# Latent attention scores from rounded values and rests: three single passes in place of one full-precision product, in a two-block transformer kernel

## The chip, the cores and the metric

The kernel runs on one core of a Trainium2 chip. Five engines work side by side: TensorE (matrix products and transposes, results into PSUM), ScalarE (one function or copy over a tile), VectorE (elementwise work and reductions), GpSimd and SyncE, which here starts the transfers of weights from memory. Each engine runs its own queue in order and waits on semaphores. The metric is the device time in microseconds of one execution.

## What is computed

Two transformer blocks of two layers each over 256 tokens of width 1024. The change touches only one part of the first block, latent attention with 8 heads whose queries and keys have 96 features (64 from a projection, 32 rotated):

```python
def latent_attention(c_q, c_kv, k_rope, w_qb, w_kvb, q_norm_g, kv_norm_g):
    q = jnp.einsum('bsr,re->bse', rms_norm(c_q, q_norm_g), w_qb).reshape(b, s, MLA_HEADS, MLA_NOPE_DIM + MLA_ROPE_DIM)
    ...
    k = jnp.concatenate([k_nope, jnp.broadcast_to(k_r, (b, s, MLA_HEADS, MLA_ROPE_DIM))], -1)
    o = blocked_attention(q, k, v, (MLA_NOPE_DIM + MLA_ROPE_DIM) ** -0.5)

def blocked_attention(q, k, v, scale):
    ...
        sc = jnp.einsum('bqhd,bkhd->bhqk', qi, k, preferred_element_type=jnp.float32) * scale
        p = jax.nn.softmax(sc, axis=-1).astype(v.dtype)
        return jnp.einsum('bhqk,bkhd->bqhd', p, v)
```

Everything is float32.

## The kernel before

Weights stream through three slots of 2048 columns. ScalarE writes each piece's rounded value (`whi`, type float32r) and VectorE the rest (`wlo` = piece minus `whi`); there are four slots of each. A weight product is then three single passes: rounded by rounded, rounded by rest, rest by rounded. ScalarE's `split_to` (L1184) waits for the transfer and for a free slot (`w_used`, given by TensorE when it has read a piece to the end); VectorE's `split_to` (L1708) waits for ScalarE.

The order on each engine is written out by hand. In the stage of the latent heads (points "ml") TensorE mixes attention with weight products. `filler` (L559) hands out a share of such products at each call of `fill`, and `mark` notes which weight products have ended there. ScalarE and VectorE call `catch` at the same points; it evicts what has ended and parts the next pieces of weights.

The heads go in groups g = 0 to 3 of two, heads 2g and 2g+1, and a fifth round finishes the last pair. Each round of TensorE is: the scores of the two heads (L835), the turn of head 2g+2 (`turn_latent`, L800: four full-precision transposes at L804, queries and keys, into 96 partitions of PSUM bank 6), products, the transposes of the probabilities of the group before (`turn_probs`, L630, at L638), products, the turn of head 2g+3, the second transposes of probabilities, products, and `mix_pair` (L641, at L648: probabilities by values). Heads 0 and 1 are turned ahead of the rounds. In the second layer the same happens again.

There is only one bank for a turned head. So `turn_latent` of a head waits for `qk_out` of the head before it, with which VectorE says that it has copied bank 6 to `qk` (L1919, buffer 0 for even heads, 1 for odd ones). The scores of a head wait for its own `qk_out` and for the exponentials that last used their bank.

VectorE in a round: `normalise_pair` of the group before (L1943), `maxima` of both heads (L1926, at L1929 and L1930), `qk_out` of head 2g+2, `catch`, `catch`, `qk_out` of head 2g+3, `catch`, and the rest of the mixed pair. ScalarE in a round: the exponentials of both heads (`exp_pair`, L1315, at L1324), `catch`, `probs_out` (L1328, at L1332: the turned probabilities out of PSUM), `catch`, `probs_out`, `catch`, `pair_hi`.

Of the kernel before, what the change touches and what calls it, by code (L numbers as in the profile page):

```python
# [11 lines left out]
ALU = mybir.AluOpType  # L12
# [50 lines left out]
    "first_sum", "windows_in", "rotated", "subln", "lam", "lam_exp",  # L63
    "qk_turned", "qk_out", "scored", "negm", "exped", "heads_out",
    "probs_in", "probs_turned", "probs_out", "heads_mixed", "pairs_mixed", "pair_hi", "pair_out",
# [4 lines left out]
Sems = namedtuple("Sems", SEMS)  # L70
Tensors = namedtuple("Tensors", [n for n, _, _ in SBUF] + ["ps", "down", "cw", "sgw", "brow", "xTh", "xTl"])
Kernel = namedtuple("Kernel", "nc t out m s raws leads free size first after call bank halves seen")
# [51 lines left out]


def by_columns(ap):

    return ap.rearrange("p (r w c) -> p w r c", r=4, w=4)
# [11 lines left out]
def build(nc, t, out):  # L140
    first, after, call, size = {}, {}, {}, []
    for name, pieces in gemm_names():
        first[name], after[name], call[name] = len(size), len(size) + len(pieces), len(call) + 1
        size += pieces
    with ExitStack() as ctx:
        sb = [ctx.enter_context(nc.sbuf_tensor(name, shape, dt)) for name, shape, dt in SBUF]
        ps = ctx.enter_context(nc.psum_tensor("ps", [P, 8, 512], F32))
        named = dict(zip([n for n, _, _ in SBUF], sb))
        flat = named["rpb"][:].rearrange("p a b c -> p (a b c)")
        m = Tensors(*sb, ps, ps[:, 4:8, :].rearrange("p (t n) w -> p t (n w)", t=2),  # L150
                    flat[:, 0:NSTEP * 16].rearrange("p (c f k) -> p c f k", c=NSTEP, f=4),
                    flat[:, D:2 * D].rearrange("p (h q) -> p h q", h=8), flat[:, 2 * D:2 * D + 640], named["xT"][:, :, 0, :], named["xT"][:, :, 1, :])
        s = Sems(*[ctx.enter_context(nc.semaphore(name)) for name in SEMS])
        k = Kernel(nc, t, out, m, s, (s.raw0, s.raw1, s.raw2), (s.lead0, s.lead1, s.lead2), (s.free0, s.free1, s.free2), size, first, after, call,
                   {}, [], {})
        tensor_program(k)
        sync_program(k)
        pool_program(k)
        scalar_program(k)
        vector_program(k)  # L160
# [240 lines left out]
def tensor_program(k):  # L401
# [282 lines left out]
    for L in range(DEPTH):  # L684
# [144 lines left out]
        for g in range(5):  # L829
            if g < 4:  # L830
                for h in (2 * g, 2 * g + 1):
                    PE.wait_ge(s.qk_out, g0 + h + 1)
                    PE.wait_ge(s.exped, h0 + 2 * g)
                    for th in range(2):
                        mm = PE.matmul(ps[:, 3 + h % 2, th * S:(th + 1) * S], m.qk[0:96, h % 2, th * P:(th + 1) * P],  # L835
                                       m.qk[0:96, h % 2, S:2 * S], start=True, stop=True)
                    mm.then_inc(s.scored, 1)
# [341 lines left out]
def scalar_program(k):  # L1179
# [135 lines left out]
    def exp_pair(h0, p_free, g, scale, biased=False, heads=(0, 1)):  # L1315

        for h in [2 * g + j for j in heads]:
# [8 lines left out]
            e.then_inc(s.exped, 1)  # L1326

    def probs_out(p0, i, m_free, width=2 * S):  # L1328
        AC.wait_ge(s.probs_turned, p0 + i + 1)
        if m_free > 0:  # L1330
            AC.wait_ge(s.pairs_mixed, m_free)
        AC.activation(m.probT[:, i % 2, 0:width], ps[:, 5, 0:width], ACT.Copy).then_inc(s.probs_out, 1)  # L1332
# [41 lines left out]
    for L in range(DEPTH):  # L1374
# [65 lines left out]

        for i in (6, 9):
            catch(1, L, "ml", "pre", i)
        blocks_hi(m.bTh, 4, 3, gain=lambda kt: m.pcol[:, 6:7])
# [3 lines left out]
        for g in range(5):  # L1447
            if g < 3:
                exp_pair(h0, p0 + 2 * g - 2, g, 96 ** -0.5)
            if g == 3:  # L1450
                exp_pair(h0, p0 + 2 * g - 2, g, 96 ** -0.5, heads=(0,))
            catch(1, L, "ml", g, 1, ahead=0 if g else SPLIT)
            if g:
                probs_out(p0, 2 * g - 2, m0 + g - 1)
            if g == 3:
                exp_pair(h0, p0 + 2 * g - 2, g, 96 ** -0.5, heads=(1,))
            catch(1, L, "ml", g, 2)
            if g:
                probs_out(p0, 2 * g - 1, m0 + g - 1)
# [238 lines left out]
def vector_program(k):  # L1698
# [217 lines left out]

    def qk_out(rows, buf):
        DV.wait_ge(s.qk_turned, n.up("groups"))
        DV.tensor_copy(m.qk[0:rows, buf, :], ps[0:rows, 6, :]).then_inc(s.qk_out, 1)  # L1919

# [89 lines left out]
    for L in range(DEPTH):  # L2010
# [65 lines left out]
        n.up("probs", 4)  # L2076
        qk_out(P, 0)
        catch(1, L, "df", "pre", 4)
# [5 lines left out]
        for g in range(5):  # L2084
# [4 lines left out]
            if g < 3:  # L2089
                qk_out(P, (g + 1) % 2)  # L2090
            if g == 4:
# [9 lines left out]
        n.up("probs", 8)  # L2101
        qk_out(96, 0)
        catch(1, L, "ml", "pre", 6)
        qk_out(96, 1)
        catch(1, L, "ml", "pre", 9)
# [9 lines left out]
        for g in range(5):  # L2115
            if g:
                normalise_pair(h0, g - 1)
            if g < 4:
                maxima(h0, g, 96 ** -0.5)
            if g < 3:  # L2120
                qk_out(96, 0)
            catch(1, L, "ml", g, 1, ahead=0 if g else SPLIT)
            catch(1, L, "ml", g, 2)
            if g < 3:
                qk_out(96, 1)
            catch(1, L, "ml", g, 3, ahead=SPLIT - 1)
            if g:
                pair_lo(g - 1)
# [380 lines left out]
```

## Time and profile before

| | before |
|---|---|
| median of 3 runs | 1452.88 us (1452.18 to 2392.74) |
| the profiled execution | 1452.48 us, span 1451.2 us |
| TensorE busy (products) | 1436.1 us, 99% |
| VectorE busy | 1040.1 us, 72% |
| ScalarE busy | 813.7 us, 56% |
| share of the transfer engines | 53.8% for the weights' queue |

A page of the profile tells how long each engine was busy in the span. Matmuls are pipelined: a row's duration runs from its start to an end that is modelled, and neighbours overlap, so what a pass takes of TensorE is read from the distance of two starts. A full-precision product appears as two records. In the time lines below times count from the start of the span.

### The profile page before, as it was taken

What the parts mean: (1) busy time and instruction counts of PE and PEld (TensorE: products, weight loads), DVE (VectorE), ACT (ScalarE), POOL (GpSimd) and SP (SyncE); (2) the same over time, 40 slices, a digit from 0 to 9 for tenths busy, and PEclk for the clock granted to TensorE, in tenths of its full rate; (3) what the DMA queues carried; (4) which work ended last, traced back from release to release, by engine and by line L of the source; (5) the groups of instructions that cost most, each with busy time, mean ns of one, the idle gap of its engine ahead of it and who ended that gap; (6) DMA issues with size and microseconds to landing.
All of it is one profiled execution on the core that took longest, in us unless ns stands there. A gap on an engine that the chain in (4) does not pass through costs nothing.

```text
span 1451.2 us, 19722 instructions
## 1 busy us (share of the span) xinstructions
PE 1436.1 (99%) x7721; PEld 1208.5 (83%) x7721; DVE 1040.1 (72%) x1423; ACT 813.7 (56%) x1177; POOL 62.2 (4%) x100
## 2 busy tenths in 40 slices
PE   8999999999999999999999999999999999999999
PEld 6788878888887888887888888788888888888888
DVE  5766876855557556875865556877988868788886
ACT  5565554354443565754454444676655657775563
POOL 1010000000001000000100000210000012000000
PEclk9999999999999999999999999999999999999999
DMA  8754635565665464642756565436556644456651
GB/s 271 250 191 147 217 131 170 171 210 183 200 212 187 156 204 133 217 147 92 254 183 219 184 198 174 147 109 209 174 189 198 217 134 160 139 177 202 197 186 58
DMA packets 172684, 261.09 MB, mean 180 GB/s; under 512 B 9520, under 2 KB 111568, under 8 KB 172336
## 3 DMA queue, kind: packets, MB, share of 16 engines
q1 hardware_dynamic: 171296, 255.18, 53.8%
q0 software_dynamic: 1152, 4.65, 0.9%
q8 instruction: 61, 1.00, 0.3%
q14 instruction: 31, 0.25, 0.1%
q10 hardware_dynamic: 144, 0.01, 0.0%
HBM read 256.66 MB, written 1.05 MB: 178 GB/s over the span
## 4 chain that ended last, share of the span: by engine, by line
PE 92%; DVE 5%; ACT 1%; POOL 1%; issue 1%; DMA 0%; DVEq 0%; ACTq 0%
PE ps L458 16%; PE ps L534 12%; PE ps L536 11%; PE ps L535 11%; PE ps L459 9%; PE ps L428 7%; PE ps L432 6%; PE ps L430 6%; PE ps L461 2%; DVE wlo L1714 1%; PE ps L835 1%; PE ps L486 1%; PE ps L638 1%; DVE bn L1721 1%; PE ps L1076 1%; DVE x L1773 1%
## 5 line engine op out<-in xcount | busy, mean ns | idle before, releaser
L1714 DVE TENSOR_TENSOR wlo<-raw,whi 128x2048 fp32r<-128x2048 f32 (+1 forms) x234 | 519.6, 2229 | 224.2 <-ACT whi L1192 224.2
L1192 ACT ACTIVATE whi<-raw 128x2048 fp32r<-128x2048 f32 (+1 forms) x234 | 434.4, 1865 | 139.9 <-PE ps L536 52.2
L458 PE MATMUL ps<-xT,whi 128*128 128x512 f32 x1008 | 356.4, 395 | 0.0
L459 PE MATMUL ps<-xT,wlo 128*128 128x256 f32 x1152 | 311.2, 280 | 0.0
L534 PE MATMUL ps<-whi,xT 128*128 128x512 f32 (+3 forms) x640 | 250.4, 391 | 2.2 <-DVE xT L1792 1.2
L536 PE MATMUL ps<-whi,xT 128*128 128x512 f32 (+3 forms) x640 | 242.0, 378 | 0.0
L535 PE MATMUL ps<-wlo,xT 128*128 128x512 f32 (+3 forms) x640 | 241.4, 377 | 0.0
L458 PEld LDWEIGHTS ps<-xT,whi 128*128 128x128 f32 x1008 | 189.0, 188 | 42.1
L459 PEld LDWEIGHTS ps<-xT,wlo 128*128 128x128 f32 x1152 | 217.4, 189 | 6.1
L534 PEld LDWEIGHTS ps<-whi,xT 128*128 128x128 f32 x640 | 120.3, 188 | 25.1 <-issue 5.2
L536 PEld LDWEIGHTS ps<-whi,xT 128*128 128x128 f32 x640 | 120.2, 188 | 22.6
L535 PEld LDWEIGHTS ps<-wlo,xT 128*128 128x128 f32 x640 | 120.6, 188 | 19.0
L428 PE MATMUL ps<-whi,aTh 128*128 128x512 f32 x300 | 93.0, 391 | 0.0
L430 PE MATMUL ps<-wlo,aTh 128*128 128x512 f32 x300 | 92.7, 390 | 0.0
L432 PE MATMUL ps<-whi,aTl 128*128 128x512 f32 x300 | 92.6, 390 | 0.0
L2370 DVE SCALAR_TENSOR_TENSOR proj<-proj,rpb 128x255 f32<-128x255 f32 x160 | 70.2, 480 | 2.2 <-ACT proj L1636 0.7
L432 PEld LDWEIGHTS ps<-whi,aTl 128*128 128x128 f32 x300 | 56.3, 188 | 12.0
L430 PEld LDWEIGHTS ps<-wlo,aTh 128*128 128x128 f32 x300 | 56.3, 188 | 11.8
L428 PEld LDWEIGHTS ps<-whi,aTh 128*128 128x128 f32 x300 | 55.7, 188 | 10.4
L1513 ACT ACTIVATE prob<-ps 128x512 f32<-128x512 f32 x36 | 21.6, 599 | 73.2 <-PE ps L461 73.2
L461 PE MATMUL ps<-xT,whi 128*128 128x512 f32 x144 | 53.8, 396 | 0.0
L1636 ACT ACTIVATE proj<-proj,rpb 128x256 f32<-128x256 f32 x80 | 43.5, 591 | 13.7 <-DVE proj L2386 11.5
(244 smaller groups left out, 1962.5 us busy)
## 6 DMA issues: line engine op xcount, KB each, us to landing
raw<-in_w_in SPq DMA_DIRECT2D x120, 512.0 KB, 4.8
raw<-in_w_ffn_in SPq DMA_DIRECT2D x88, 512.0 KB, 4.9
raw<-in_w_up SPq DMA_DIRECT2D x88, 512.0 KB, 4.8
raw<-in_w_ffn_out SPq DMA_DIRECT2D x44, 512.0 KB, 4.4
raw<-in_w_down SPq DMA_DIRECT2D x44, 512.0 KB, 4.5
raw<-in_w_branch SPq DMA_DIRECT2D x24, 512.0 KB, 4.8
raw<-in_w_out SPq DMA_DIRECT2D x16, 512.0 KB, 4.2
raw<-in_w_o SPq DMA_DIRECT2D x16, 512.0 KB, 4.6
```

The lines of the kernel that those rows point to most:

```text
L428: PE.matmul(o, ah, hi[:, j, b], start=first and kt == 0, stop=False)
L430: PE.matmul(o, ah, lo[:, j, b], start=False, stop=False)
L432: mm = PE.matmul(o, al, hi[:, j, b], start=False, stop=last and j == c - 1 and i == len(kts) - 1)
L458: PE.matmul(ps[:, b, :], hi, m.xT[:, kt], start=kt == 0, stop=False)
L459: mm = PE.matmul(ps[:, b, 0:S], lo, m.xTh[:, kt], start=False, stop=False)
L461: mm = PE.matmul(ps[:, b, :], hi, m.xT[:, kt], start=False, stop=True)
L534: PE.matmul(o, ah, hi[:, j, :], start=kt == 0, stop=False)
L535: PE.matmul(o, ah, lo[:, j, :], start=False, stop=False)
L536: mm = PE.matmul(o, al, hi[:, j, :], start=False, stop=end)
L1192: AC.activation(m.whi[:, i % SPLIT, 0:w], m.raw[:, slot, 0:w], ACT.Copy).then_inc(s.w_hi, 1)
L1714: DV.tensor_tensor(m.wlo[:, i % SPLIT, 0:w], m.raw[:, slot, 0:w], m.whi[:, i % SPLIT, 0:w].bitcast(F32), ALU.subtract).then_inc(s.w_lo, 1)
L2370: a = DV.scalar_tensor_tensor(out=conv[:, f, to], in0=src[:, f, of], scalar=m.cw[:, c, f, tap:tap + 1], in1=conv[:, f, to], op0=ALU.mult, ...
```

## The change

The copy of a turned head by VectorE is replaced by two steps. ScalarE copies bank 6 as float32r, which rounds it, into `lath` (`latent_hi`), and gives the new semaphore `qk_hi`. VectorE waits for that and writes the bank minus the rounded value into `latl` (`latent_lo`), then gives `qk_out`, as its copy did. `lath` lies where `qk` lay, `latl` in the half of `rpb` that held the values of the neighbourhood heads. Each product of the scores (128 queries by 256 keys, in full precision) becomes three single passes: rounded queries by rounded keys, rest of queries by rounded keys, rounded queries by rest of keys. The product of the two rests is left out, as in the weight products.

```diff
@@ tensor_program, latent heads
                 for h in (2 * g, 2 * g + 1):
                     PE.wait_ge(s.qk_out, g0 + h + 1)
                     PE.wait_ge(s.exped, h0 + 2 * g)
+                    hi, lo = latent_parts(m, h % 2)
                     for th in range(2):
-                        mm = PE.matmul(ps[:, 3 + h % 2, th * S:(th + 1) * S], m.qk[0:96, h % 2, th * P:(th + 1) * P],
-                                       m.qk[0:96, h % 2, S:2 * S], start=True, stop=True)
+                        o, qh = ps[:, 3 + h % 2, th * S:(th + 1) * S], hi[:, th * P:(th + 1) * P]
+                        PE.matmul(o, qh, hi[:, S:2 * S], start=True, stop=False)
+                        PE.matmul(o, lo[:, 0, th, :], hi[:, S:2 * S], start=False, stop=False)
+                        mm = PE.matmul(o.rearrange("p (t s) -> p t s", t=2), qh, lo[:, 1], start=False, stop=True)
                     mm.then_inc(s.scored, 1)
@@ scalar_program
+    def latent_hi(buf):
+
+        h = n.up("latent")
+        AC.wait_ge(s.qk_turned, h + 8 * ((h + 7) // 8))
+        AC.activation(latent_parts(m, buf)[0], ps[0:96, 6, :], ACT.Copy).then_inc(s.qk_hi, 1)
+
@@ scalar_program, latent heads
-        for i in (6, 9):
-            catch(1, L, "ml", "pre", i)
+        latent_hi(0)
+        catch(1, L, "ml", "pre", 6)
+        latent_hi(1)
+        catch(1, L, "ml", "pre", 9)
...
             if g == 3:
                 exp_pair(h0, p0 + 2 * g - 2, g, 96 ** -0.5, heads=(0,))
+            if g < 3:
+                latent_hi(0)
             catch(1, L, "ml", g, 1, ahead=0 if g else SPLIT)
...
             catch(1, L, "ml", g, 2)
+            if g < 3:
+                latent_hi(1)
             if g:
                 probs_out(p0, 2 * g - 1, m0 + g - 1)
@@ vector_program
+    def latent_lo(buf):
+
+        n.up("groups")
+        hi, lo = latent_parts(m, buf)
+        DV.wait_ge(s.qk_hi, n.up("qk_hi"))
+        DV.tensor_tensor(lo, ps[0:96, 6, :].rearrange("p (a t s) -> p a t s", a=2, t=2),
+                         hi.bitcast(F32).rearrange("p (a t s) -> p a t s", a=2, t=2), ALU.subtract).then_inc(s.qk_out, 1)
@@ vector_program, latent heads: the four calls
-                qk_out(96, 0)
+                latent_lo(0)
```

On ScalarE the new copy stands behind the four exponentials of a group. This is the first group of the first layer before, from the exponentials (`prob<-ps,negm`) over the gate (`gate<-gate`) and a piece of weights (`whi<-raw`) to the exponentials of the next group:

```order
L1324 ACTIVATE prob,rs<-ps,negm 128x256 [waits probs_turned,negm]
L1324 ACTIVATE prob,rs<-ps,negm 128x256
L1324 ACTIVATE prob,rs<-ps,negm 128x256 [waits probs_turned,negm]
L1324 ACTIVATE prob,rs<-ps,negm 128x256
L1291 ACTIVATE gate<-gate 128x512 [waits free2]
L1192 ACTIVATE whi<-raw 128x2048 [waits w_used,raw2]
```

The same place in the changed kernel:

```order
L1337 ACTIVATE prob,rs<-ps,negm 128x256 [waits probs_turned,negm]
L1337 ACTIVATE prob,rs<-ps,negm 128x256
L1337 ACTIVATE prob,rs<-ps,negm 128x256 [waits probs_turned,negm]
L1337 ACTIVATE prob,rs<-ps,negm 128x256
L1345 ACTIVATE lath<-ps 96x512 [waits qk_turned]
L1304 ACTIVATE gate<-gate 128x512 [waits free2]
L1345 ACTIVATE lath<-ps 96x512 [waits qk_turned]
L1205 ACTIVATE whi<-raw 128x2048 [waits w_used,raw2]
```

The copy of head 2 has come in between the exponentials and the gate, that of head 3 between the gate and the weights. In group 2 of the changed kernel the copy stands ahead of the probabilities' copy (`probT<-ps`) and of the weights:

```order
L1337 ACTIVATE prob,rs<-ps,negm 128x256 [waits probs_turned,negm]
L1337 ACTIVATE prob,rs<-ps,negm 128x256
L1345 ACTIVATE lath<-ps 96x512 [waits qk_turned]
L1351 ACTIVATE probT<-ps 128x512 [waits pairs_mixed,probs_turned]
L1205 ACTIVATE whi<-raw 128x2048 [waits w_used,raw1]
L1345 ACTIVATE lath<-ps 96x512 [waits qk_turned]
L1351 ACTIVATE probT<-ps 128x512 [waits pairs_mixed,probs_turned]
```

On VectorE nothing moves; the copy of bank 6 becomes a subtraction in the same place. In group 0 of the first layer it stood between the maxima and the gate's addition, before:

```order
L1929 TENSOR_REDUCE negm<-ps 128x2 [waits scored]
L1930 TENSOR_SCALAR negm<-negm 128x2 [waits dve_step]
L1919 COPY qk<-ps 96x512 [waits qk_turned]
L1849 TENSOR_TENSOR gate<-ps,vec 128x512 [waits th0_sum,gate_b]
L1919 COPY qk<-ps 96x512 [waits qk_turned]
```

and now:

```order
L1962 TENSOR_REDUCE negm<-ps 128x2 [waits scored]
L1963 TENSOR_SCALAR negm<-negm 128x2 [waits dve_step]
L1951 TENSOR_TENSOR latl<-ps,lath 96x4x128 [waits qk_hi]
L1874 TENSOR_TENSOR gate<-ps,vec 128x512 [waits th0_sum,gate_b]
L1951 TENSOR_TENSOR latl<-ps,lath 96x4x128 [waits qk_hi]
```

What it waits for is now ScalarE (`qk_hi`) and no longer TensorE (`qk_turned`).

## Rows read from the trace of the kernel before

**Rows 1.** The page's busy times: engine, us, share of the span, instructions.
```profile
PE 1436.1 (99%) x7721; PEld 1208.5 (83%) x7721; DVE 1040.1 (72%) x1423; ACT 813.7 (56%) x1177; POOL 62.2 (4%) x100
```

**Rows 2.** The chain that ended last, share of the span by engine.
```profile
PE 92%; DVE 5%; ACT 1%; POOL 1%; issue 1%; DMA 0%; DVEq 0%; ACTq 0%
```

**Rows 3.** TensorE's waits for weight rests: us in total, times, longest.
```profile
PE ps L534 <- DVE wlo L1714: 0.4, 1, 0.4
```

**Rows 4.** Window, length, busy us of PE, PEld, DVE, ACT, POOL; clock, transfers.
```profile
177.00:217.00 40.00, 40.00 (x208) 32.05 (x208) 31.74 (x55) 20.90 (x48) 0.00 (x0) 1.00 0.40 132
```

**Rows 5.** TensorE's time line (start, us, line, out<-in, xcount), head 3, group 1.
```profile
183.52 0.60 PE L804 MATMUL ps<-ident,proj 128*96 128x128 f32 x4
...
186.02 1.89 PE L835 MATMUL ps<-qk 96*128 96x256 f32 x8
187.75 0.60 PE L804 MATMUL ps<-ident,proj 128*96 128x128 f32 x4
```

**Rows 6.** Time line, single passes of 256 columns in the second block.
```profile
1150.54 0.28 PE L453 MATMUL ps<-xT,whi 128*128 128x256 f32 x1
1150.55 0.19 PEld L454 LDWEIGHTS ps<-xT,wlo 128*128 128x128 f32 x1
1150.66 0.28 PE L454 MATMUL ps<-xT,wlo 128*128 128x256 f32 x1
...
1150.78 0.28 PE L455 MATMUL ps<-xT,whi 128*128 128x256 f32 x1
```

**Rows 7.** Time line of VectorE and ScalarE, end of group 0's exponentials.
```profile
182.04 0.68 DVE L1919 COPY qk<-ps 96x512 f32<-96x512 f32 x1
...
183.09 0.21 ACT L1324 ACTIVATION_READ_ACCUMULATOR prob<-ps,negm 128x1 f32 x1
183.10 0.69 DVE L1849 TENSOR_TENSOR gate<-ps,vec 128x512 f32<-128x512 f32 x1 [0.38 <-PE ps L536]
...
183.83 0.63 ACT L1291 ACTIVATE gate<-gate 128x512 f32<-128x512 f32 x1 [0.52 <-DVE gate L1849]
```

**Rows 8.** Time line, a transpose that waited for VectorE.
```profile
150.50 0.88 DVE L1960 SCALAR_TENSOR_TENSOR prob<-prob,ri 128x256 f32<-128x256 f32 x2
...
151.44 0.66 PE L638 MATMUL ps<-ident,prob 128*128 128x128 f32 x4
```

**Rows 9.** Time lines of the three engines, group 2 and scores of group 3.
```profile
202.85 0.21 ACT L1324 ACTIVATION_READ_ACCUMULATOR prob<-ps,negm 128x1 f32 x1
202.94 0.61 ACT L1332 ACTIVATE probT<-ps 128x512 f32<-128x512 f32 x1
...
203.70 0.60 PE L804 MATMUL ps<-ident,proj 128*96 128x128 f32 x4
...
205.38 2.29 DVE L1714 TENSOR_TENSOR wlo<-raw,whi 128x2048 fp32r<-128x2048 f32 x1 [1.59 <-ACT whi L1192]
...
207.75 1.99 PE L835 MATMUL ps<-qk 96*128 96x256 f32 x8
...
210.96 0.39 PE L534 MATMUL ps<-whi,xT 128*128 128x512 f32 x1
211.19 0.39 PE L535 MATMUL ps<-wlo,xT 128*128 128x512 f32 x1
```

**Rows 10.** Time lines of the three engines, group 1 and scores of group 2.
```profile
189.80 0.21 ACT L1324 ACTIVATION_READ_ACCUMULATOR prob<-ps,negm 128x1 f32 x1
...
192.79 0.60 PE L804 MATMUL ps<-ident,proj 128*96 128x128 f32 x4
...
196.69 0.68 DVE L1919 COPY qk<-ps 96x512 f32<-96x512 f32 x1
196.84 1.99 PE L835 MATMUL ps<-qk 96*128 96x256 f32 x8
```

**Rows 11.** Second layer, the two rows that answer to group 2 above.
```profile
649.92 0.61 ACT L1332 ACTIVATE probT<-ps 128x512 f32<-128x512 f32 x1
...
650.67 0.60 PE L804 MATMUL ps<-ident,proj 128*96 128x128 f32 x4
```

## Prediction: where TensorE gains, and where it waits for the copy

> **What bounds the kernel now.** I read the page's busy times first: TensorE is busy 1436.1 us, 99% of the span [rows 1]. The chain that ended last is 92% TensorE [rows 2]. So the time is the sum of what TensorE runs, plus the moments in which it stands still: work taken from TensorE shortens the run, work added to another engine costs nothing until TensorE waits for it. Next I read the waits of TensorE: the largest one for weight rests is 0.4 us, once [rows 3]. Last I read the time of the latent heads: from 177 to 217 us TensorE is busy 40.00 of 40.00 us, VectorE 31.74, ScalarE 20.90, at a granted clock of 1.00, the upper level of 2.4 GHz [rows 4]. TensorE can't be filled further here, VectorE has little room, ScalarE has room on average. What matters is when ScalarE is free, since a new step on it now stands between a transpose and the scores.
>
> **Scores: less TensorE work.** There are 4 groups of two heads in each of 2 layers, 8 groups. A group's four full-precision products are eight records, and from the first of them (186.02) to the transposes behind them (187.75) it takes 1.73 us [rows 5]. After the change a group is 2 heads x 2 halves x 3 = 12 single passes of 128x256 with a weight load each. The same kind of run stands in the second block: passes at 1150.54, 1150.66 and 1150.78, so 0.12 us each [rows 6]. 12 x 0.12 = 1.44, a gain of 0.29 us a group, 2.3 us in all. The floor of a pass is half of a record of the present scores, since two passes lie in each record of 1.73/8 = 0.216 us: 0.108, which would gain 0.43 a group, 3.5 in all. I take 0.12, because the loads lie beside it there as they will here. A pass of single precision behind full-precision work starts no later than a full-precision one does, so I book nothing for the switch (at most 0.1 a group, 0.8 in all).
>
> **One rule that speaks against it.** The rows show a load beginning at 1150.55, 0.01 us after the product ahead of it began, and lasting 0.19, while products go on every 0.12 [rows 6]: loads lie beside products. The Trainium skill, in "TensorE: Matmul & The Clock Gate", section "The mechanism", says that a weight load overlaps running matmuls only where the row groups differ, which they don't here. Twelve loads in place of eight would then be a loss. The trace does not agree, so the sum goes by 0.12.
>
> **Parting: what is added.** VectorE copied a 96x512 bank in 0.68 us [rows 7]. Now it subtracts, reading the bank and the rounded value; the row nearest to that is the 128x512 addition out of PSUM, 0.69 [rows 7]. Its work doesn't change, by these two (bounds 0.6 and 0.9: a third more for writing in pieces of 128 columns, which no row shows). ScalarE gets 16 copies of 96x512 from PSUM. The copy of 128x512 out of PSUM takes 0.61 [rows 9]; I take 0.60, bounds 0.5 and 0.8 (the same spread). As work this is hidden (ScalarE 20.90 of 40). As a step in a chain it isn't: the bank is read by ScalarE first, VectorE waits for that, and TensorE may not turn the next head until the rest is written.
>
> **Where the copy comes too late: group 0.** ScalarE executes in order, and the copy of head 2g+2 is queued behind the four exponentials of group g. In group 0 TensorE turned head 3 at 183.52 [rows 5]; VectorE had copied head 2 at 182.04 to 182.72 [rows 7], so nobody waited. Now: the last read of the exponentials starts at 183.09 [rows 7], and the next ScalarE instruction follows 0.09 behind such a read (202.85 to 202.94 [rows 9]), so at 183.18. The exponentials don't move, since VectorE's maxima ahead of them stand behind weight rests. The copy ends at 183.78, the rest goes from 183.81 to 184.50, and TensorE starts 0.06 behind the end of what it waits for (VectorE ends 150.50 + 0.88, TensorE starts 151.44 [rows 8]): 184.56. It would have been ready at 183.52 - 0.29 = 183.23. **Stall 1.33 us**, and TensorE is now 1.04 later than before.
>
> Is anything behind that late too? On VectorE the gate addition of 183.10 comes at 184.42, ScalarE's gate of 183.83 at 185.15 [rows 7], and the copy of head 3 behind it ends at 186.26, its rest at 186.98. Scores of group 1 are due at 186.02 + 1.04 = 187.06: just covered, by 0.02. In group 1, where TensorE is 1.04 late up to the scores and 0.75 behind them, the exponentials end at about 191.0 (189.80 + 0.21 [rows 10], plus 1.04), the rest of head 4 at 192.3, and TensorE turns head 5 at 192.79 + 0.75 = 193.54 [rows 10]. Covered by 1.2 us. The rest of head 5 stands behind two weight rests, as its copy did (196.69 [rows 10]), and moves with TensorE by 0.75: it ends at 198.12. The scores of group 2, 196.84 before [rows 10], start at 197.59 with head 4 and want head 5 at 197.59 + 0.72 = 198.31. Covered by 0.13.
>
> **Group 2.** TensorE is 1.04 - 0.29 - 0.29 = 0.46 later than before and turns head 7 at 203.70 + 0.46 = 204.16 [rows 9]. VectorE has been running without a pause and carries its 0.75 of delay, so the exponentials' last read starts at 202.85 + 0.75 = 203.60 [rows 9]; the copy runs 203.69 to 204.29, the rest to 205.00, TensorE starts at 205.05. **Stall 0.89 us.** Behind it ScalarE has the probabilities' copy (202.94 before, now 204.2) and then the weights' rounded piece, so the weight rest of 205.38 comes 1.24 later [rows 9]. Who waits for that piece? It is the first of the second gate half; TensorE opens the half ahead of it at 210.96 and spends 48 passes of 0.23 us on it (210.96 to 211.19), so it is wanted from 222 on, and there are some 13 us. The rest of head 7 comes right behind that weight rest (205.38 + 1.24 + 2.2 = 208.8) and ends at 209.5, and its scores are due at 207.75 + 1.35 + 0.72 = 209.8 [rows 9]. Covered. Group 3 parts no heads and gives 0.29 back. After the latent heads VectorE and ScalarE have pauses in which they catch up, but TensorE has none, and what it lost stays lost.
>
> **Sum.** A layer: -4 x 0.29 + 1.33 + 0.89 = +1.06 us. The second layer runs the same order at the same distances: TensorE's turn of head 7 at 650.67 and ScalarE's copy at 649.92 [rows 11] stand 446.97 and 446.98 behind those of rows 9. So twice: **+2.1 us** (gain 2.3, stalls 4.4). The profiled execution took 1452.48 us, 1.3 more than its span; the median of the runs is 1452.88. 1452.88 + 2.1 = 1455.0.
>
> **Rivals.**
> 1. *The copy is in time, the gain stays.* That wants ScalarE's copy and VectorE's rest to be done 1.3 us sooner in group 0. Against it: the exponentials start only at VectorE's negated maxima, which don't move, and the queue is fixed. For it: only that TensorE's waits are read from ends that are modelled. Time: 1452.9 - 2.3 = 1450.6, with the floor of 0.108 a pass 1449.4. This is the case of a gain.
> 2. *More stalls than two.* Covers of 0.02 (scores of group 1) and 0.13 (head 5's scores) are thin. If the copy takes 0.8 and the rest 0.9, each of the two stalls grows by 0.4 and the scores of group 1 wait 0.4: 1.2 a layer more, 1457.4. With the other cover gone as well (0.3) and 0.1 at each switch of precision it is 1459 to 1460.
> 3. *Loads don't lie beside these passes* (the slow side beyond 2%). A pass would take 0.19 + 0.12 = 0.31, a group 3.7 us in place of 1.73, 8 x 2.0 = 16 us more, 1469 without stalls and about 1473 with them. From 0.48 us a pass on (1.73 + 4 us a group) it would be slower by over 2%. Against it stand rows 6. The rule of the Trainium skill named above would put the run on this side; by the same page's figures (sections "LDWEIGHTS (loading the stationary operand)" and "Back-to-back issue gap": 107 ns for 128 columns of weights, 109 ns for 256 columns of product) a group would be estimated at 12 x 0.216 = 2.6 us.
> 4. *Nothing can be told*: gain and stalls cancel, 1452.9.
>
> **How the numbers follow.** Forecast with two stalls a layer (1453.5 to 1457) 0.60; rival 2 0.17; rival 1 0.14; rival 4 0.06; rival 3 0.03. The range of 1451.0 to 1459.5 leaves out most of rival 1, rival 3 and the end of rival 2. 2% is 29 us, about what a measurement of this kernel can tell from no change: all cases but the far end of rival 3 lie within it. Faster by over 2% 0.005, within 0.985, slower 0.01.
>
> **What the changed profile would show.** The twelve passes of a group over 1.44 us, 0.12 apart. TensorE's weight load of the turns of heads 3 and 7 idle before it for 1.3 and 0.9 us, released by VectorE's subtraction, in both layers, and no such wait at heads 1, 2, 4, 5, 6. ScalarE's copy at about 0.60, the subtraction at about 0.69, and VectorE waiting for ScalarE some 1 to 2 us ahead of the subtractions of heads 2, 4 and 6. I would be wrong if the turn of head 3 had no wait (then the time is near 1452 or under), if waits stood ahead of the scores themselves, or if passes stood 0.2 apart.

## The result, and the profile after

The changed kernel takes 1455.21 us (median of 15 runs, 1454.72 to 1456.57), the kernel before 1452.31 (median of 15). The ratio is 1.0021, 95% interval 1.0014 to 1.0028: 2 to 4 us more, 3.0 as the ratio has it. One run of the kernel before took 2392.74 us, far outside the rest, and is left out of the ratio; why it did is not known. The profiled execution took 1455.96 us with a span of 1454.6.

The page's busy times after (engine, us, share of the span, instructions), and the chain that ended last:

```profile
PE 1435.4 (99%) x7753; PEld 1209.6 (83%) x7753; DVE 1040.3 (72%) x1423; ACT 820.9 (56%) x1193; POOL 62.2 (4%) x100
PE 88%; DVE 7%; ACT 2%; issue 1%; DMA 1%; POOL 1%; SPq 0%; DVEq 0%; ACTq 0%
```

TensorE has 32 products more (8 groups x 12 passes in place of 8 records) and is busy 0.7 us less than in [rows 1]. That 0.7 is not the gain of the passes: rows that end in a wait run on into it by their modelled ends, so each of the two stages of latent heads shows 0.7 us less (43.00 us before, 42.3 after), and the first 15 us of the two runs differ by 0.5 the other way. The gain is read from starts, below. The chain's share of VectorE rose from 5% to 7% and that of TensorE fell from 92% to 88% [rows 2]. TensorE's waits (engine, out, line, who it waited for: us in total, times, longest) name the place:

```profile
PE ps L690 <- DMA rope<-in_rope: 6.4, 1, 6.4
PE ps L814 <- DVE latl L1951: 3.8, 4, 1.2
PE ps L496 <- DVE x L1798: 2.4, 7, 0.8
PE ps L438 <- DVE xT L1805: 0.7, 1, 0.7
```

The first and the third are in the kernel before too, with 6.7 and 2.4 us. The second is new: four waits of the turn of a head for the rest of the head before it ("rest" is the bank minus its rounded value). So is the fourth, once. The scores of group 0, TensorE's time line:

```profile
177.39 0.28 PE L847 MATMUL ps<-lath 96*128 96x256 f32 x1
177.51 0.28 PE L848 MATMUL ps<-lath,latl 96*128 96x256 f32 x1
177.63 0.28 PE L849 MATMUL ps<-latl,lath 96*128 96x256 f32 x1
...
178.71 0.28 PE L849 MATMUL ps<-latl,lath 96*128 96x256 f32 x1
178.83 0.60 PE L814 MATMUL ps<-ident,proj 128*96 128x128 f32 x4
```

Twelve passes from 177.39 to 178.83: 1.44 us, 0.12 apart, against 1.73 in [rows 5]. The end of that group's exponentials and what follows on the three engines, where TensorE had not waited before [rows 5, rows 7]:

```profile
183.27 0.21 ACT L1337 ACTIVATION_READ_ACCUMULATOR prob<-ps,negm 128x1 f32 x1
183.37 0.59 ACT L1345 ACTIVATE lath<-ps 96x512 fp32r<-96x512 f32 x1
183.99 0.69 DVE L1951 TENSOR_TENSOR latl<-ps,lath 96x512 fp32r<-96x512 f32 x1 [1.68 <-ACT lath L1345]
184.60 0.68 DVE L1874 TENSOR_TENSOR gate<-ps,vec 128x512 f32<-128x512 f32 x1
184.74 0.64 PE L814 MATMUL ps<-ident,proj 128*96 128x128 f32 x4 [1.19 <-DVE latl L1951]
```

ScalarE's copy starts 0.10 behind the last read of the exponentials, VectorE has waited 1.68 us for it, TensorE 1.19. The exponentials themselves have not moved: that read starts at 183.27, against 183.09 in [rows 7], and the whole run is 0.18 later there. The same in group 2, where it answers to [rows 9]:

```profile
203.90 0.59 ACT L1345 ACTIVATE lath<-ps 96x512 fp32r<-96x512 f32 x1
204.38 0.60 ACT L1351 ACTIVATE probT<-ps 128x512 f32<-128x512 f32 x1
204.52 0.69 DVE L1951 TENSOR_TENSOR latl<-ps,lath 96x512 fp32r<-96x512 f32 x1 [1.67 <-ACT lath L1345]
205.26 0.65 PE L814 MATMUL ps<-ident,proj 128*96 128x128 f32 x4 [0.70 <-DVE latl L1951]
```

To see where the time went, I set the start of each TensorE instruction beside that of the same instruction before ("shift", after minus before; it is worked out from the two traces' time lines). The two runs differ by 0.18 us ahead of the latent heads already.

| place | shift ahead of it and behind it, layer 1 | layer 2 |
|---|---|---|
| scores of group 0 | 0.18, -0.11 | 2.19, 1.93 |
| turn of head 3 | -0.11, 1.26 | 1.93, 3.29 |
| scores of group 1 | 1.26, 0.98 | 3.29, 3.00 |
| scores of group 2 | 0.98, 0.69 | 3.00, 2.72 |
| turn of head 7 | 0.69, 1.61 | 2.72, 3.64 |
| scores of group 3 | 1.61, 1.32 | 3.64, 3.33 |
| mix of the third pair (216.79 before) | 1.32, 1.41 | 3.33, 3.45 |

Each layer costs some 1.25 us (0.18 to 1.41, and 2.19 to 3.45). Group 0 of the scores gives 0.29, the turn of head 3 takes 1.36 to 1.37, groups 1 and 2 give 0.29 each, the turn of head 7 takes 0.92. Between the two layers' latent heads, at 282 us, TensorE loses 0.7 to 0.8 us more, which is the fourth wait above. ScalarE and TensorE there:

```profile
278.88 1.92 ACT L1205 ACTIVATE whi<-raw 128x2048 fp32r<-128x2048 f32 x1 [5.38 <-DMA raw<-in_w_ffn_in]
282.05 0.50 PE L438 MATMUL ps<-whi,xT 128*128 128x512 f32 x1 [0.68 <-DVE xT L1805]
```

A piece of weights landed when ScalarE had waited 5.38 us for it, 7.2 us after its transfer was started, against 5.6 us in the run of before; a step of VectorE that the product needs stood behind that piece. The experiment e7 below runs the same kernel again, and there the piece is in time: the loss belongs to this execution, and not to every one of the changed kernel.

### The profile page after: what moved, and what is told of

Read it like the earlier page. It is cut to its first block, busy times and chain, and to the rows that moved or that the text cites. A ratio compares the mean times of both kernels' runs of the same rounds, so it can differ in the third digit from the quotient of the medians.

```text
span 1454.6 us, 19802 instructions
## 1 busy us (share of the span) xinstructions
PE 1435.4 (99%) x7753; PEld 1209.6 (83%) x7753; DVE 1040.3 (72%) x1423; ACT 820.9 (56%) x1193; POOL 62.2 (4%) x100
## 4 chain that ended last, share of the span: by engine, by line
PE 88%; DVE 7%; ACT 2%; issue 1%; DMA 1%; POOL 1%; SPq 0%; DVEq 0%; ACTq 0%
PE ps L468 16%; PE ps L544 11%; PE ps L546 11%; PE ps L545 10%; PE ps L469 9%; PE ps L438 7%; PE ps L442 6%; PE ps L440 6%; PE ps L471 2%; DVE wlo L1739 2%; PE ps L496 1%; PE ps L1089 1%; DVE bn L1746 1%; PE ps L648 1%; PE ps L598 1%
```

## The experiments

Nine experiments ran. Each edit is against the changed kernel, but for the last, and e7 is the changed kernel as it is; "before" was measured anew beside each set: 1452.35 us (median of 28 runs) beside e1 to e4, 1452.16 (25) beside e5 to e8, 1452.31 (15) beside e9.

My theory: the loss is the two turns that wait, since ScalarE's copy stands behind the exponentials (the prediction's stalls), and the gain of the three passes is there in full beneath it. Its rival: the three passes gain nothing, or the parting itself costs, wherever it stands.

### e1: the copy ahead of the exponentials

```diff
             if g < 3:
+                latent_hi(0)
                 exp_pair(h0, p0 + 2 * g - 2, g, 96 ** -0.5)
...
-            if g < 3:
-                latent_hi(0)
             catch(1, L, "ml", g, 1, ahead=0 if g else SPLIT)
```

> The changed kernel with one edit: ScalarE's copy of head 2g+2 stands ahead of the four exponentials of group g, not behind them; all work is the same. Theory A (the copy is late because it is queued behind the exponentials): the waits of TensorE at the turns of heads 3 and 7 (1.19 and 0.70 us on TensorE's row, each in both layers) are gone, the gain of 0.29 us a group stays, and perhaps 0.15 us a layer is lost at the scores of head 7. Time 1452.3 - 2.0 = 1450.3. Theory B (reading the bank twice, one engine behind the other, is what costs, wherever the copy stands): the two stalls stay at more than half their size, time 1453.5 to 1455.2. Theory C (the copy moved ahead makes the exponentials late by up to 0.6 us and the scores of the next group or the transposes of probabilities wait in place of the turns): waits under other names, time 1452 to 1455.

Measured: 1451.46 us (1451.21 to 1452.07), ratio 0.9994 (0.9986 to 1.0003). The waits at the turns are gone and the gains of 0.29 stay at groups 0 to 2, so the theory stands on its place: 3.75 us lie between this kernel and the changed one. Against the kernel before its interval reaches over 1. At group 3 only 0.16 to 0.17 of the 0.29 is left: the first pass of head 7 starts at 207.70, 0.06 behind the end of its rest (206.96 + 0.68), and the next one 0.22 later and not 0.12. That is the 0.15 that the expectation had allowed. But 1450.3 was expected. Of the 1.06 us that layer 1 had gained by group 3, 0.42 went again, at a place that the prediction had not looked at, and as much in layer 2. TensorE waits (twice, once in each layer) at the mix of the third pair:

```profile
PE ps L658 <- ACT probT L1351: 0.7, 2, 0.4
```

and the time line there shows ScalarE and TensorE:

```profile
213.68 1.94 ACT L1205 ACTIVATE whi<-raw 128x2048 fp32r<-128x2048 f32 x1
215.48 0.61 ACT L1351 ACTIVATE probT<-ps 128x512 f32<-128x512 f32 x1
216.15 1.08 PE L658 MATMUL ps<-probT,proj 128*64 128x256 f32 x8 [0.36 <-ACT probT L1351]
```

The second copy of the probabilities stands behind a piece of weights of 1.94 us. In the kernel before it stood there too:

```profile
216.13 0.61 ACT L1332 ACTIVATE probT<-ps 128x512 f32<-128x512 f32 x1
216.79 1.08 PE L648 MATMUL ps<-probT,proj 128*64 128x256 f32 x8
```

It ended at 216.74 and TensorE started at 216.79, the 0.05 to 0.06 behind its releaser that a start takes: no wait and no slack. In e1 TensorE comes 1.06 us earlier and the copy only 0.65 (216.13 to 215.48), so TensorE waits for the difference.

### e2 and e3: the parting without the passes, the passes without the parting

e2 keeps both steps of the parting and takes the scores in full precision; e3 takes the three passes, all of rounded by rounded, and has one rounding copy on VectorE, where the old copy stood, and nothing on ScalarE. Both leave out the products with the rests, so their scores are less exact; only their times are of use.

```diff
@@ e2, tensor_program
-                        PE.matmul(o, qh, hi[:, S:2 * S], start=True, stop=False)
-                        PE.matmul(o, lo[:, 0, th, :], hi[:, S:2 * S], start=False, stop=False)
-                        mm = PE.matmul(o.rearrange("p (t s) -> p t s", t=2), qh, lo[:, 1], start=False, stop=True)
+                        mm = PE.matmul(o, qh.bitcast(F32), hi[:, S:2 * S].bitcast(F32), start=True, stop=True)
@@ e3, tensor_program
-                        PE.matmul(o, lo[:, 0, th, :], hi[:, S:2 * S], start=False, stop=False)
-                        mm = PE.matmul(o.rearrange("p (t s) -> p t s", t=2), qh, lo[:, 1], start=False, stop=True)
+                        PE.matmul(o, qh, hi[:, S:2 * S], start=False, stop=False)
+                        mm = PE.matmul(o, qh, hi[:, S:2 * S], start=False, stop=True)
@@ e3, vector_program, latent_lo
-        DV.wait_ge(s.qk_hi, n.up("qk_hi"))
-        DV.tensor_tensor(lo, ps[0:96, 6, :].rearrange("p (a t s) -> p a t s", a=2, t=2),
-                         hi.bitcast(F32).rearrange("p (a t s) -> p a t s", a=2, t=2), ALU.subtract).then_inc(s.qk_out, 1)
+        DV.wait_ge(s.qk_turned, n.up("groups"))
+        DV.tensor_copy(latent_parts(m, buf)[0], ps[0:96, 6, :]).then_inc(s.qk_out, 1)
```

> The changed kernel with both steps of the parting kept, but the scores taken in full precision as before, from the rounded values alone (the rests are written and not read, so that part of the products is left out). Theory A: only the stalls are left. At the turn of head 3 TensorE is due 0.29 us later than in the changed kernel, so the stall there is 1.05 us in place of 1.34, and at the turn of head 7 about 0.65 in place of 0.9; with 0.05 a restart some 1.8 to 1.9 a layer, time 1452.3 + 3.7 = 1456.0. Theory B (the twelve single passes themselves cost more than they show, by their 12 weight loads or the switch of precision): with the old products back the time falls to 1452.3 to 1454.

> The twelve single passes alone: VectorE rounds the bank in one copy as it copied it before, ScalarE has no part in it, and all three passes read the rounded values (the rests are left out). Theory A: the gain alone, 0.29 us a group, with up to 0.15 us a layer lost at the scores of head 7, whose copy is then late: 1452.3 - 2.0 to 2.3 = 1450.0 to 1450.3, and no wait at any turn. Theory B (passes cost more than they show): 1452.3 or more.

Measured: e2 1455.91 us (1455.67 to 1456.09), ratio 1.0024 (1.0015 to 1.0034); e3 1451.60 us (1451.03 to 1452.33), ratio 0.9994 (0.9985 to 1.0003). e2 came out as expected: with no gain from the passes the kernel is 3.6 us over the one before. Its shift goes from 0.06 to 1.13 over the turn of head 3 and to 1.78 over the turn of head 7, and its waits sum to less than in the changed kernel (2.7 us against 3.8), since TensorE, which gains nothing, reaches each turn later:

```profile
PE ps L814 <- DVE latl L1949: 2.7, 4, 0.9
```

A layer moves TensorE by 1.72 us here (0.06 to 1.78) and by 1.23 in the changed kernel (e7 below). The difference of some 0.5 is what the passes bring there; they gain 4 x 0.29 = 1.15. So some 0.65 us a layer of the gain only makes waits longer: 0.29 at the turn of head 3 (all that group 0 gains), 0.28 at the turn of head 7, and 0.08 at the mix of the third pair. Ahead of a waiting turn the releaser's queue sets the time, and TensorE's own work doesn't, or only in part.

e3 missed its number by 1.3 to 1.6 us, in the way of e1: the same two waits of 0.7 us in all at the mix of the third pair. As e3 has no copy on ScalarE at all, that wait is not made by the copy ahead of the exponentials (theory C of e1); and as e1 and e3 lie 0.14 us apart, e1's copies on ScalarE cost nothing that these runs can tell.

### e4 and e5: one copy twice

The copy of one head is done twice on ScalarE (the first into a place that nobody reads): that of head 2 in e4, that of head 4 in e5.

```diff
         AC.wait_ge(s.qk_turned, h + 8 * ((h + 7) // 8))
+        if h % 8 == 3:
+            AC.activation(m.latl[0:96, 4:6, :, P:S], ps[0:96, 6, :].rearrange("p (a t s) -> p a t s", a=2, t=2), ACT.Copy)
         AC.activation(latent_parts(m, buf)[0], ps[0:96, 6, :], ACT.Copy).then_inc(s.qk_hi, 1)
```

(`h` counts one ahead; e5 has 5 in place of 3.)

> The changed kernel with ScalarE's copy of head 2 made twice (the first into rows that nobody reads), once a layer. Theory A (the copy is on the path there, one for one): the second costs its step of 0.5 us, the wait at the turn of head 3 grows from 1.2 to 1.7 us in both layers, everything behind it moves along, time 1455.2 + 1.0 = 1456.2. Theory B (something else ends the wait last): the wait stays, 1455.2.

> The changed kernel with ScalarE's copy of head 4 (group 1) made twice (the first into rows that nobody reads), once a layer. Theory A (the copy costs only where its cover is used up; at head 4 the rest was done 1.2 us before the turn of head 5 was due): no wait at the turn of head 5, the waits at heads 3 and 7 as in the changed kernel, time that of the changed kernel within 0.3 us, 1455.2. Theory B (each ScalarE instruction put in costs its length wherever it stands): 1455.2 + 1.0 = 1456.2, as the same doubling at head 2 did (1456.48).

Measured: e4 1456.48 us (1455.84 to 1456.79), ratio 1.0027 (1.0016 to 1.0038), as expected. The turn of head 3 moves TensorE by 1.81 us in place of 1.33, so a copy on the path costs what ScalarE's queue gives it, 0.48 us from start to start, not the 0.60 of its row. The median lies 1.27 over the changed kernel, of which the two copies are 0.97; the profiled execution (1456.48 too) also lost 0.5 us at a late piece of weights in layer 2, the place named above, so that the time came out near 1456.2 is in part chance. The waits:

```profile
PE ps L814 <- DVE latl L1953: 4.7, 4, 1.7
```

e5 1455.55 us (1455.35 to 1455.95), ratio 1.0023 (1.0014 to 1.0033), 0.64 more than the changed kernel beside it; within 0.3 was expected. The turn of head 5 does not wait, as the prediction's 1.2 us of cover says, but the wait of head 7 grew. VectorE and TensorE in e5:

```profile
192.58 0.69 DVE L1953 TENSOR_TENSOR latl<-ps,lath 96x512 fp32r<-96x512 f32 x1 [2.27 <-ACT lath L1347]
193.19 0.68 DVE L1876 TENSOR_TENSOR gate<-ps,vec 128x512 f32<-128x512 f32 x1
193.79 2.28 DVE L1741 TENSOR_TENSOR wlo<-raw,whi 128x2048 fp32r<-128x2048 f32 x1
...
194.06 0.60 PE L814 MATMUL ps<-ident,proj 128*96 128x128 f32 x4
...
205.81 0.64 PE L814 MATMUL ps<-ident,proj 128*96 128x128 f32 x4 [0.90 <-DVE latl L1953]
```

and in the changed kernel, profiled again (e7):

```profile
192.48 0.69 DVE L1874 TENSOR_TENSOR gate<-ps,vec 128x512 f32<-128x512 f32 x1 [0.18 <-PE ps L546]
...
205.10 0.64 PE L814 MATMUL ps<-ident,proj 128*96 128x128 f32 x4 [0.70 <-DVE latl L1951]
```

e5's run is 0.50 us later than e7's from its start on. The gate's addition had 0.18 us of pause ahead of it; that is used up, and in e5 it is 0.71 later, so 0.21 later than the start accounts for. All of VectorE's queue behind it has no pause up to the maxima of group 2, and those release the exponentials, so the 0.21 is carried to the copy of head 6. TensorE's wait there is 0.20 longer, in each layer. A cover that is read at the next wait of TensorE alone is read too short: the delay went on in another queue and came out at the turn after. That is 0.4 us of the 0.64 between the medians; the other 0.24 are not explained.

### e6: the second bound taken away too

e1's edit, and in group 3 ScalarE's second copy of the probabilities goes ahead of its piece of weights, and VectorE normalises the last pair ahead of its rest of the weights.

```diff
@@ scalar_program, with e1's edit
                 exp_pair(h0, p0 + 2 * g - 2, g, 96 ** -0.5, heads=(1,))
+                probs_out(p0, 2 * g - 1, m0 + g - 1)
             catch(1, L, "ml", g, 2)
...
-            if g:
+            if g and g != 3:
                 probs_out(p0, 2 * g - 1, m0 + g - 1)
@@ vector_program
-            if g:
+            if g and g < 4:
                 normalise_pair(h0, g - 1)
...
             catch(1, L, "ml", g, 1, ahead=0 if g else SPLIT)
+            if g == 3:
+                normalise_pair(h0, 3)
             catch(1, L, "ml", g, 2)
```

> The kernel with the copy ahead of the exponentials, and in group 3 two things more: ScalarE's second copy of turned probabilities stands ahead of the piece of weights, and VectorE normalises the last pair ahead of its piece of weights. The trace of the kernel with the copy first shows TensorE waiting 0.36 us, in both layers, at the values' product of the third pair for that probabilities' copy, which stands behind a piece of weights of 1.94 us. Theory A (this queue is the next bound, with no slack already before, and it takes back a third of the gain): the wait of 0.36 goes, 0.42 us a layer come back, 1451.5 - 0.8 = 1450.6, under the kernel before by 1.7. Theory B (the chain through VectorE's maxima sets the end of group 3 whatever is queued): another wait of the same size takes its place, 1451.5.

Measured: 1450.65 us (1450.27 to 1452.06), ratio 0.9991 (0.9982 to 1.0000), the lowest of all. In its trace the shift against the kernel before is -0.07 ahead of the latent heads, -1.09 behind those of layer 1 and -2.07 behind those of layer 2, with no new wait. Group 3 of layer 1:

```profile
213.73 0.60 ACT L1351 ACTIVATE probT<-ps 128x512 f32<-128x512 f32 x1
214.22 1.91 ACT L1205 ACTIVATE whi<-raw 128x2048 fp32r<-128x2048 f32 x1
215.70 1.08 PE L658 MATMUL ps<-probT,proj 128*64 128x256 f32 x8
```

The mix starts 1.09 us earlier than at 216.79 before, without a wait. This is nearly the change's whole gain of 2.3 us: 2.0 us in the trace, 1.5 between the medians. What the trace lacks is the 0.12 a layer at the scores of head 7, as in e1 (here the passes start at 207.68 and 207.90). The interval's upper end is 1.0000, so by the medians it is only just told from nothing; the trace's shifts, which name each place, say more.

### e7: the changed kernel again

> The changed kernel as it is, a second profile. Its first profile lost 0.67 us at a weight piece of the feed-forward stage that landed 7.2 us after its transfer was started, where 5.6 is seen in the kernel before. Theory A (that landing varies from execution to execution and the change has no part in it): the four waits at heads 3 and 7 are the same within 0.05 us, the 0.67 is not there in this profile or stands in another layer, and the time is 1455.2. Theory B (the change moved that transfer into a worse place): the same piece lands late again.

Measured: 1454.91 us (1454.64 to 1455.76), ratio 1.0019 (1.0011 to 1.0028). The late piece of weights did not recur: that piece was taken at 276.98 after 3.65 us of waiting, and the loss at 281 is absent. The waits at the turns are the same within 0.02 us each (3.7 us over the four):

```profile
PE ps L814 <- DVE latl L1951: 3.7, 4, 1.2
```

The shift is 0.01 ahead of the latent heads of layer 1, 1.24 behind them and 2.47 behind those of layer 2: 2.46 in all, where the prediction's sum was 2.1. It accounts for the two profiled executions to the end: 1454.91 - 1452.48 = 2.43. One more profile does not show that the change leaves the transfer alone. At this place, in both layers of all eleven profiles, 17 pieces were taken 5.3 to 5.6 us after the start of their transfer and five 6.2 to 7.2 us after it, all five in kernels with the new passes; TensorE lost 0.68, 0.42 and 0.06 us at the three latest of them. The kernels without the passes (before, e2, e9) have only six such places between them, too few to tell.

### e8: both steps on VectorE

Nothing on ScalarE (`latent_hi` is empty); VectorE rounds bank 6 and then subtracts.

```diff
@@ vector_program, latent_lo
-        n.up("groups")
         hi, lo = latent_parts(m, buf)
-        DV.wait_ge(s.qk_hi, n.up("qk_hi"))
+        DV.wait_ge(s.qk_turned, n.up("groups"))
+        then(DV.tensor_copy(hi, ps[0:96, 6, :]))
```

> The parting done by VectorE alone: it rounds the bank (0.60 us more a head) and then subtracts; ScalarE has no part in it, the result is the same. Theory A (what costs is the place behind ScalarE's exponentials): the wait at the turn of head 3 falls to 0.15 us, and VectorE's added 0.6 us a head shows later instead, about 0.35 at head 7's turn and 0.5 to 0.9 at its scores and at the values' product of the third pair; 1452.3 - 2.3 + 2.4 = 1452 to 1454. Theory B (any second step on the way from a turn to the scores costs as much as ScalarE's): 1455 or more.

Measured: 1457.24 us (1456.69 to 1457.83), ratio 1.0035 (1.0022 to 1.0047): over the expected range, and the slowest of all. By its number alone theory B ("1455 or more") would stand. The trace speaks for A at the place in question: TensorE's wait at the turn of head 3 is 0.13 us by its rows, where 0.15 was expected and the changed kernel has 1.19.

```profile
183.97 0.39 PE L546 MATMUL ps<-whi,xT 128*128 128x512 f32 x1
184.49 0.64 PE L814 MATMUL ps<-ident,proj 128*96 128x128 f32 x4
```

What costs is elsewhere:

```profile
PE ps L847 <- DVE latl L1949: 2.1, 4, 0.7
PE ps L524 <- DVE proj L2141: 1.7, 2, 0.8
PE ps L658 <- ACT probT L1349: 0.7, 2, 0.4
```

The first is what I had expected in kind (VectorE, with 31.74 of 40 us taken [rows 4], has little room for 0.6 to 0.7 us more a head, and now the scores wait for it). The second I had not, and it moves TensorE by over 0.9 us a layer: the steps of heads 0 and 1 push the last step of another part of the attention, the product that its norm gives, ahead of which VectorE has no pause.

```profile
170.60 0.68 DVE L1872 TENSOR_TENSOR gate<-ps,vec 128x512 f32<-128x512 f32 x1
171.20 1.21 DVE L2141 TENSOR_TENSOR proj<-proj,small 128x1024 f32<-128x1024 f32 x1
172.47 1.09 PE L524 MATMUL ps<-ident,proj 128*128 128x128 f32 x8 [0.85 <-DVE proj L2141]
```

Before, that step ran at 169.86 and TensorE turned its output at 171.56 without a wait. So in this kernel the rounding is better on ScalarE, if it has the right place in the queue: e1 and e8 lie 5.8 us apart. Other places for both steps on VectorE were not tried.

### e9: the kernel before, with the probabilities first

The kernel before with only the reorder of group 3 from e6, no parting.

> The kernel before with one edit: in group 3 ScalarE copies the second half of the probabilities ahead of its piece of the weights, and VectorE normalises that pair ahead of its rest of the weights; no parting of queries and keys. Theory: in the kernel before TensorE reaches the mix of the third pair just when the copy of its probabilities ends (0.00 to 0.01 us of slack, no wait), so the reorder has nothing to give: 1452.2 us, ratio 1.000 within 0.001. What the reorder gave in the kernel with the early copies (1450.65 against 1451.46, 0.8 us) was then given because those kernels came there a microsecond earlier. Rival: the reorder is a gain of its own, whatever stands before it: 1451.4 us, ratio 0.9994.

Measured: 1452.34 us (1452.00 to 1452.86), ratio 1.0000 (0.9991 to 1.0009). The reorder is worth nothing by itself. The trace's shift is constant through the latent heads of both layers. What it gives in e6 over e1 (0.8 us between the medians and in the traces, 0.6 with each set against the kernel before beside it) it gives because TensorE comes there earlier.

## Why the prediction held, point by point

**The time.** 1455.0 was predicted as the time itself, 2.1 us over before; measured are 1455.21 and 1454.91, which is 2.9 and 2.75 over the medians beside them. 1455.0 was built on a median of three runs (1452.88); with the later medians (1452.16 to 1452.35) the same sum would have given 1454.4. So the difference was predicted 0.6 to 0.8 us too small, and that is the honest measure of the sum; that 1455.0 and 1455.21 lie so near is in part luck, a base 0.6 too high and a difference 0.6 to 0.8 too small. Two sizes beside the sum were off too. "2% is 29 us, about what a measurement can tell" is far too coarse: the interval of the ratio is 0.0014 wide, 2 us. And rival 3 would be slower by over 2% from 0.45 us a pass on ((1.73 + 29/8)/12), not 0.48.

**Gain of the passes, 0.29 us a group: right.** 1.44 for twelve passes, shifts of -0.26 to -0.31 at the eight groups. The switch of precision was booked at nothing. Rival 3 (loads not beside passes) fell: the load at 187.29 begins with the pass at 187.29 and lasts 0.19, passes go on 0.12 apart. The load's row even runs 0.07 past the start of the pass that needs it, so its length is not to be taken at its word; the spacing of the passes is. By the rule of the Trainium skill that the prediction weighed ("TensorE: Matmul & The Clock Gate", section "The mechanism") they would not lie beside each other; this trace doesn't agree either. The same section also says that a load may be pulled ahead when it goes to a background weight buffer, which the prediction did not weigh and which would fit these rows; no run here shows which it is.

```profile
187.29 0.28 PE L847 MATMUL ps<-lath 96*128 96x256 f32 x1
187.29 0.19 PEld L848 LDWEIGHTS ps<-lath,latl 96*128 96x128 f32 x1
187.41 0.28 PE L848 MATMUL ps<-lath,latl 96*128 96x256 f32 x1
```

**Copy 0.60 and subtraction 0.69: right** (0.59 and 0.69; the subtraction's pieces of 128 columns cost nothing). In ScalarE's queue the copy takes only 0.48, from 203.90 to 204.38.

**Stalls of 1.33 and 0.89 us: right in place, 0.04 short in size.** The first transpose of the turn of head 3 moved from -0.11 to 1.22 (1.33), the next one stands at 1.26; for head 7 it is 0.69 to 1.57 (0.88), then 1.61. So each of the four restarts costs 0.04 beyond the wait, which the sum lacks; e2's four do the same (1.09 to 1.13, 1.74 to 1.78). All waits that it excluded (heads 1, 2, 4, 5 and 6, the scores) are absent.

**The thin covers of 0.02 and 0.13: they held.** The scores of group 1 started at 187.29 without a wait, 0.14 us after the rest of head 3 ended (186.46 + 0.69); with the 0.06 that a start takes, the cover was 0.08. The passes of head 5 started at 198.64, 0.30 after its rest ended at 198.34, a cover of 0.24.

**The cover of the turn of head 5, 1.2 us: right, but read too short.** e5 took 0.48 of it, and 0.21 came out at the turn of head 7. The step "covered, so free" failed as a method, not as a number.

**"The weight rest comes later, and there are 13 us": right** for TensorE. But the sentence "Group 3 parts no heads and gives 0.29 back" left out the mix of the third pair, where ScalarE's copy had no slack. It cost 0.08 to 0.12 a layer here, since both engines came there late, ScalarE a little more than TensorE. In rival 1 the omission weighs most: 1450.6 was given for "the copy is in time". The copies in time (e1) gave 1451.46, and 1450.65 only with the second bound taken away (e6). That this meets 1450.6 is luck again: beside e6 the kernel before took 1452.16, so the rival's sum would give 1449.9.

**The account.** The prediction's 2.12, four restarts of 0.04 and two mixes of 0.08 to 0.12 make 2.4 to 2.5; e7's trace has 2.46. The medians beside e7 differ by 2.75; the profiled execution of before lay 0.3 over the median beside e7, and that is the whole of what is left, smaller than the spread of the runs. What makes the piece of weights land 5.6 or 7.2 us after its start stays open, and so does whether the change makes the late case more frequent.

## What to carry to other kernels

A faster product pays only as far as the queues that feed it run ahead. Ask for each waiting instruction what its releaser stands behind, and follow the releaser back to the instruction that starts its chain. Here a step of 0.48 us behind four exponentials cost 4.6 us in four waits, and the same step ahead of them cost nothing that could be told. When one bound is removed, look for the next one among the places where the trace shows no wait and no slack: take the end of every releaser and the start of its waiter, and ask how much earlier the releaser would come in its own queue. What the waiter gains beyond that and the slack is lost: here TensorE came 1.06 us earlier, its releaser 0.65, and 0.4 went.

A cover has to be followed through every queue that the late instruction stands in, to that queue's next pause, and not only to the next wait of the busiest engine.

## What the runs showed that I had not expected

- A restart of TensorE behind a wait of 0.45 to 1.2 us costs about 0.04 us more than the wait, within the transposes behind it.
- ScalarE's instructions overlap: a copy whose row lasts 0.59 us is followed by the next 0.48 us after its start, an overlap of 0.11. The Trainium skill ("ScalarE: Activation LUTs", section "What ACT_TABLE_LOAD costs") puts the overlap of ACTIVATEs back to back at about 93 ns; the trace agrees roughly.
- The same transfer of a piece of weights landed 5.6 and 7.2 us after its start in two runs, and 0.7 us of TensorE hung on it; over all profiles and both layers five of 22 came later than 6 us.
